# RWKV projections of keys, receptance, gate and values in products of Strassen's kind on one Trainium2 core

## The chip, the core and the metric

The kernel runs on one core of one Trainium2 chip. The metric is device time in microseconds, the median of three runs. Beside the runs there is one profiled execution, from which every trace row comes.

## The reference, cut to what matters

One step of a two-layer decoder. Layer 0 is an RWKV-7 layer; its input projection is what the change touches:

```python
proj = concat([prev_xn, xn]) @ w_in               # 1024 -> r, k, v (768 each), w/a LoRA, memory query, gate
mixed = cur + (proj[:, :-1, :n_sh] - cur) * mu     # token shift, for r, k, v
kk = k * k_k;  kk = kk / max(|kk|, 1e-12)          # per head of 64
k = k * (1 + (a - 1) * k_a)
S_t = S_{t-1} (diag(decay) - kk^T (kk a)) + v^T k;  o_t = S_t r_t
y = concat([norm(o) + bonus * v, memory]) * silu(gate);  h = h + y @ w_out
```

There are 1024 prompt tokens, 8 samples of 8 tokens and 8 carried rows, so the turned input `xT` is 128 partitions x 8 blocks of the 1024 inputs x 1096 columns (1024 + 64 + 8). All data are float32. After layer 0 come shared keys and values, a second layer of attention and the sample attention; the change does not touch them.

## The kernel before

`rwkv_pairs` handles the 12 heads as 6 pairs (`PAIRS`), each pair on the 128 partitions. A pair p has two phases on TensorE (PE), written out by hand:

- `middle(p)`: turn the values (`turn_tokens(0, vT)`), wait for `prep_ready`, then the decay products (line 833), which VectorE (DVE) masks, then five levels of small products that invert the chunks' triangular matrices.
- `recurrence(p)`: 16 steps n, one for each chunk of 64 tokens, a loop of dependences. In a step PE multiplies the state (line 1003), ScalarE (ACT) copies the result out as `r_sb` (line 1156), PE multiplies it (line 1020), DVE copies that out as `sa_sb` (line 1362), PE makes the next state (lines 1032 and 1033), and DVE writes it as `xs` (line 1368).

Between these dependent products PE fills in the projections of the next pair. The projections are a list of `PIECES`, each cut into `PARTS` (one matrix product of 128 inputs), dealt evenly over 48 slots, three to a step: slots 3n and 3n+1 follow line 1020's product, slot 3n+2 follows the new state's.

```python
PIECES = "W0 A0 K0 W1 A1 K1 W2 A2 K2 R0 R1 H0 R2 H1 V0 H2 V1 V2 G0 G1 G2".split()
                    fill(p + 1, 3 * n)
                    fill(p + 1, 3 * n + 1)
```

K, R, V, G are keys, receptance, values and gate, 8 parts each for the columns 0 to 384, 384 to 768 and 768 to 1096 (`COL3`); W and A are the two LoRA products; H sums squares for the norm of the keys. Each piece has one of four PSUM banks (piece i bank 4 + i % 4), and `wait_read` makes PE wait until the piece four before it has been read. ACT and DVE read the pieces in `feed(q, n)`, which each engine calls once at the end of step n: on ACT behind the copy of `r_sb` of step n, on DVE behind `xs` of step n (and at n == 7 behind the work of line 1380). In it ACT scales a piece by `mu` into `prev` (lines 1066 to 1070), and DVE adds the shifted columns (`mixed`, lines 1205 and 1207). Further work of `feed` stands at fixed n: the scan (line 1249) at 5, exponentials at 7, norms at 11 to 14, and at n == 15 the last two operations (lines 1275 and 1276), which raise `prep_ready`. SyncE (SP) loads the weights, 512 KB for each of K, R, V, G, into two halves of `w`: K and V into half 0, R and G into half 1. The first pair's projections run alone, ahead of `middle(0)`; pairs and recurrences are counted from 0, so recurrence 1 (312.6 to 405 us) fills in pair 2's projections; the last pair's recurrence fills in a list `TAIL` of other projections.

Of the kernel before, what the change touches and what calls it, by code (L numbers as in the profile page):

```python
# [14 lines left out]
F32 = mybir.dt.float32  # L15
# [5 lines left out]
P = 128  # L21
# [30 lines left out]
def make_constants():  # L52
# [27 lines left out]
    keep = np.ones(TT)  # L80
    keep[0:SEQ:HS] = 0
    keep[SEQ::TS] = 0
    put("keep", np.broadcast_to(keep, (P, TT)))
# [463 lines left out]
PIECES = "W0 A0 K0 W1 A1 K1 W2 A2 K2 R0 R1 H0 R2 H1 V0 H2 V1 V2 G0 G1 G2".split()  # L547
PARTS = [(i, k) for i, name in enumerate(PIECES) for k in range(KC if name[0] in "KRVG" else 1)]
# [20 lines left out]
def ended(step):  # L569

    return ended_in(step, FILL, PARTS, lambda i: KC - 1 if PIECES[i][0] in "KRVG" else 0)

# [6 lines left out]
def rwkv_pairs(nc, w_in, state_d, new_state_p, new_state_s, const, vecs, rows, omu, xT, wide, bank, lora, up, w, mq, y_m, y_last, y_d):  # L579
# [8 lines left out]
    with Stage(nc, "rwkv") as st:  # L588
# [9 lines left out]
        arT = st.sb("arT", [P, 2, NCHUNK, 2, CH])  # L598
# [28 lines left out]
        w_loaded = [st.sem(f"w_loaded{i}") for i in range(2)]  # L627
        (s0_loaded, hv_ready, piece_done, prev_ready, mix_read, th_read, h_read, g_tanh, gate_read, sq_ready, sig_ready,
# [61 lines left out]
        def _(sp):  # L690
            for q in range(PAIRS):
                for i, job in enumerate(JOBS):
                    if 4 * q + i < 2:
                        continue
                    qq, j = divmod(4 * q + i - 2, 4)
                    sp.wait_ge(piece_done, NPIECE * qq + PIECES.index(JOBS[j] + "2") + 1)
# [50 lines left out]
        def _(pe):  # L747
# [3 lines left out]
            def wait_read(q, i):  # L751
                kind, j = PIECES[i][0], int(PIECES[i][1])
                if kind in "KRV":
                    pe.wait_ge(mix_read, 9 * q + 3 * "KRV".index(kind) + j + 1)
# [4 lines left out]
                else:  # L759
                    pe.wait_ge(gate_read, 3 * q + j + 1)  # L760
# [2572 lines left out]
```

## Time and profile before

| | us |
|---|---|
| median of 3 runs | 2054.27 (2053.07 to 2056.26) |
| the profiled execution's own time | 2057.22 |
| its span, first to last instruction | 2055.3 |
| PE busy | 1912.8 (93%) |
| DVE busy | 963.2 (47%) |
| ACT busy | 635.1 (31%) |
| mean granted TensorE clock | 0.981 |

The RWKV stage lies between 77 us and about 937 us of the span: the first pair's projections from 77 to 142.5, then six times a middle of about 40 us and a recurrence of about 92 us. Busy shares are those of each engine; an engine's queue is served in its own order, so what counts is what is queued ahead of an instruction that PE needs.

### The profile page before, as it was taken

To read this page: it belongs to the slowest core of one execution; us is meant where nothing else is said; L and a number is where in the kernel's file an instruction comes from. 1 tells how busy PE (TensorE), PEld (TensorE's weight loads), DVE (VectorE), ACT (ScalarE), POOL (GpSimd) and SP (SyncE) were. 2 spreads that over 40 slices of the span, in tenths; PEclk is the share of its full clock that TensorE was granted. 3 is DMA by queue.
4 is the path that set the end of the run, shared out by engine and by line. 5 is a ranking of instruction groups with operands and counts; after the bars stand their busy time and mean duration, and the time that the engine had idled before them with its cause. 6 is when DMAs were issued, how large, how long until landed. Compare 5 with 4: busy or idle time off the path is not lost. (4 is left out here: it accounts for less than half of the span.)

```text
span 2055.3 us, 44993 instructions
## 1 busy us (share of the span) xinstructions
PE 1912.8 (93%) x19534; PEld 1314.8 (64%) x19534; DVE 963.2 (47%) x2083; ACT 635.1 (31%) x1499; POOL 305.1 (15%) x286
## 2 busy tenths in 40 slices
PE   6999989999999899897998999999999899799997
PEld 3577575675765757654443699995556566566664
DVE  4354373553734636332323476585233788633332
ACT  6322322222222223121224323232323566511111
POOL 0100030020300302111001010100010566201010
PEclk9999999999999999999999999999999999799998
DMA  8010010010100101007102130210200100667662
GB/s 290 18 37 3 22 34 23 18 39 22 34 23 12 45 22 34 24 17 263 57 1 107 53 116 32 96 52 11 92 22 11 62 1 1 236 201 231 214 223 77
DMA packets 53943, 147.70 MB, mean 72 GB/s; under 512 B 11587, under 2 KB 21123, under 8 KB 52468
## 3 DMA queue, kind: packets, MB, share of 16 engines
q1 hardware_dynamic: 43764, 103.97, 14.9%
q0 software_dynamic: 9984, 40.87, 5.7%
q8 instruction: 154, 2.52, 0.5%
q14 instruction: 41, 0.34, 0.1%
HBM read 123.58 MB, written 21.24 MB: 70 GB/s over the span
## 5 line engine op out<-in xcount | busy, mean ns | idle before, releaser
L772 PE MATMUL psum<-xT,rw_w 128*128 128x384 f32 (+1 forms) x1152 | 401.2, 487 | 0.0
L772 PEld LDWEIGHTS psum<-xT,rw_w 128*128 128x128 f32 x1152 | 205.7, 190 | 115.7 <-issue 10.7
L1368 DVE SCALAR_TENSOR_TENSOR rwkv_xs<-psum,rwkv_pc,rwkv_xsc 128x64 f32<-128x64 f32 x90 | 25.6, 284 | 225.2 <-PE psum L1033 225.2
L740 POOL DMA_DIRECT2D out<-rwkv_s x6 | 5.8, 960 | 638.5 <-ACT rwkv_out_p L1178 638.5
L1156 ACT COPY rwkv_r_sb<-psum 128x64 f32<-128x64 f32 x96 | 20.3, 212 | 258.4 <-PE psum L1003 256.0
L1625 PE MATMUL psum<-xT,gate_w 128*128 128x384 f32 (+1 forms) x288 | 97.3, 488 | 1.9 <-PEq L169 1.9
L1549 PE MATMUL psum<-xT,y_r 128*128 128x512 f32 (+1 forms) x180 | 87.2, 617 | 8.4 <-DMA y_r<-gated 8.4
L2904 PE MATMUL psum<-V,yT 128*128 128x512 f32 x192 | 92.7, 604 | 0.0
L3106 ACT COPY xT<-psum 128x384 f32<-128x384 f32 x64 | 30.5, 476 | 169.1 <-PE psum L3015 169.1
L3140 DVE COPY xT<-psum 128x384 f32<-128x384 f32 x64 | 35.6, 556 | 95.1 <-PE psum L3015 95.0
L919 PE MATMUL psum<-rwkv_dd,rwkv_am 64*64 64x64 f32 x1968 | 67.7, 219 | 9.8 <-issue 9.7
L1625 PEld LDWEIGHTS psum<-xT,gate_w 128*128 128x128 f32 x288 | 54.0, 195 | 35.0 <-issue 9.2
L2604 PE MATMUL psum<-KT,QT 64*128 64x512 f32 (+3 forms) x336 | 61.4, 479 | 14.1 <-ACT xT L2655 12.7
L919 PEld LDWEIGHTS psum<-rwkv_dd,rwkv_am 64*64 64x64 f32 x1968 | 62.8, 135 | 10.8 <-issue 10.8
L3015 PEld LDWEIGHTS psum<-base,kp 128*128 128x128 f32 x384 | 47.6, 148 | 34.1 <-issue 26.4
L1362 DVE COPY rwkv_sa_sb<-psum 128x64 f32<-128x64 f32 x96 | 21.6, 225 | 98.8 <-PE psum L1020 97.9
L801 PE MATMUL psum<-xT,rw_w 128*128 128x384 f32 (+1 forms) x192 | 66.7, 484 | 0.0
L1337 DVE TENSOR_TENSOR rwkv_mm<-psum,masks 128x256 f32<-128x256 f32 (+1 forms) x132 | 49.1, 396 | 33.1 <-PE psum L919 31.2
L1147 ACT COPY rwkv_dd<-psum 128x256 f32<-128x256 f32 (+1 forms) x108 | 37.1, 355 | 87.7 <-PE psum L934 69.2
L3015 PE MATMUL psum<-base,kp 128*128 128x128 f32 x384 | 57.4, 289 | 6.8 <-ACT xT L3106 3.9
L2615 PE MATMUL psum<-V,xT 128*128 128x128 f32 x432 | 62.5, 289 | 1.3 <-ACT xT L2677 1.3
L2615 PEld LDWEIGHTS psum<-V,xT 128*128 128x128 f32 x432 | 53.9, 193 | 12.7 <-issue 8.5
(514 smaller groups left out, 4136.3 us busy)
## 6 DMA issues: line engine op xcount, KB each, us to landing
kp<-in_cache_k SPq DMA_DIRECT2D x64, 384.0 KB, 4.0
xT<-in_cache_v POOLq DMA_DIRECT2D x48, 384.0 KB, 4.3
rw_w<-in_w_in SPq DMA_DIRECT2D x28, 512.0 KB, 3.6
gate_w<-in_cache_v POOLq DMA_DIRECT2D x16, 384.0 KB, 5.7
front_w<-in_mem_w_kv SPq DMA_DIRECT2D x2, 2048.0 KB, 14.5
x_rows<-in_x_p SPq DMA_DIRECT2D x8, 512.0 KB, 13.9
h<-in_x_p SPq DMA_DIRECT2D x8, 512.0 KB, 12.8
residual<-h POOLq DMA_DIRECT2D x8, 512.0 KB, 2.9
```

Of the source, the lines that this page charges most:

```text
L772: mm = pe.matmul(out, w[:, load % 2, k, :], xT[:, k, a:b], start=(k == 0), stop=(k == KC - 1))
L801: mm = pe.matmul(out, w[:, load % 2, k, :], xT[:, k, a:b], start=(k == 0), stop=(k == KC - 1))
L919: mm = pe.matmul(level_bank(g)[d, u, :], am[d, n, 0, :], dd[d, n, :], start=True, stop=True)
L1147: nc.scalar.copy(dd[:, group(g), :], level_bank(g)).then_inc(d_ready, 1)
L1337: nc.vector.tensor_tensor(mm_[:, group(g), :], level_bank(g), bcast(const_view(const, f"pair{b}").unsqueeze(1), [P, n, CH]), ALU.mult).the ...
L1549: mm = pe.matmul(self.bank[0:r, 5 + 2 * (u % 2), :], self.ys[k][:, n * P:n * P + r], self.w[:, k, half * 512:(half + 1) * 512], start=(k = ...
L1625: mm = pe.matmul(out, self.w[:, c % 2, k, :], self.xT[:, k, a:b], start=(k == 0), stop=(k == KC - 1))
L2604: mm = pe.matmul(both(m, is_big)[:, c, a:b], QT[d, h, i * P:(i + 1) * P], KT[d, h, a:b], start=True, stop=True)
L2615: mm = pe.matmul(bank[:, 7, 0:P], wT[:, j * P:(j + 1) * P], V[:, j, h * P:(h + 1) * P], start=(j == 0), stop=(j == i))
L2904: mm = pe.matmul(self.out(u), self.ys[k][:, n * P:(n + 1) * P], self.w[k][:, half * 512:(half + 1) * 512], start=(k == 0), stop=(k == KC - 1))
L3015: mm = pe.transpose(bank[:, 4 + half, i * P:(i + 1) * P], kp[:, g % KR, (H3 * half + i) * P:(H3 * half + i + 1) * P], ident[:, :])
L3140: nc.vector.tensor_copy(kT[:, g % TR, 1, :], bank[:, 5, 0:H3 * P]).then_inc(dve_out, 1)
```

## The change

For the first 768 tokens the pair (K, R), and then the pair (G, V), is computed as one 2 x 2 block product. The blocks are the two matrices on one side, by halves of the 1024 inputs, and on the other side the halves of the inputs by the two column ranges 0 to 384 and 384 to 768. Seven products of four parts each (X0 to X6, then Y0 to Y6) take the place of four plain pieces of eight parts each: 28 parts for 32. The columns from 768 on stay plain pieces (K2, R2, V2, G2). Sums of input blocks (`token_sums`) are made once; sums of weight blocks (`weight_sums`, `first_sum`) once for each product set and pair. Seven additions a set (`joins`) put the PSUM results together in SBUF.

The token shift of K, R and V for the 768 columns then runs from SBUF, after X6 or Y6, 768 columns at a time (`scaled_sums` on ACT, `mixed_sums` on DVE), and so do the gate's tanh and product. To make room, `arT` has one copy in place of two (its last chunks are written at n == 15), `masked` one half in place of two, the scan's mask is written anew for each pair, the keys and values of the memory (`mkT`, `mv`) are stored to DRAM at the start and loaded back at the end, and the block X12 of `xT`, which is overwritten by a difference, too.

```diff
-PIECES = "W0 A0 K0 W1 A1 K1 W2 A2 K2 R0 R1 H0 R2 H1 V0 H2 V1 V2 G0 G1 G2".split()
-PARTS = [(i, k) for i, name in enumerate(PIECES) for k in range(KC if name[0] in "KRVG" else 1)]
+PIECES = ("K2 R2 " + " ".join(f"X{j}" for j in range(7)) + " W0 A0 W1 A1 W2 A2 V2 H0 H1 H2 " + " ".join(f"Y{j}" for j in range(7)) + " G2").split()
+DEPTH_OF = {**{c: KC for c in "KRVG"}, **{c: KC // 2 for c in "XY"}}
+PARTS = [(i, k) for i, name in enumerate(PIECES) for k in range(DEPTH_OF.get(name[0], 1))]
...
         @block.sync
+            for d, t in zip(lent_d, lent):
+                sp.dma_start(d, t).then_inc(lent_out, 16)
+            sp.dma_start(lent_d[2].rearrange("p (k c) -> p k c", k=KH), X12).then_inc(lent_out, 16)
...
-                    qq, j = divmod(4 * q + i - 2, 4)
-                    sp.wait_ge(piece_done, NPIECE * qq + PIECES.index(JOBS[j] + "2") + 1)
+                    sp.wait_ge(piece_done, piece(q, "X6") if i >= 2 else piece(q - 1, ("Y6", "G2")[i]))
...
+                if i == 1:
+                    sp.wait_ge(lent_out, 48)
+                    sp.dma_start(X12, lent_d[2].rearrange("p (k c) -> p k c", k=KH)).then_inc(lent_back, 16)
+                    for d, t in zip(lent_d, lent):
+                        sp.dma_start(t, d).then_inc(lent_back, 16)
...
         @block.tensor
+                elif kind in "XY" and j == 0:
+                    pe.wait_ge(copied, 2 * q + 1 + "XY".index(kind))
+                elif kind in "XY":
+                    pe.wait_ge(joined, 14 * q + 7 * "XY".index(kind) + READ_BY[j])
...
+                    if k == 0 and j == 1:
+                        pe.wait_ge(sums_ready, 1)
+                        pe.wait_ge(factors_ready, n + 1)
+                    if k == 0 and j == 5:
+                        pe.wait_ge(first_ready, n + 1)
+                    left, right = product(kind, j, k)
+                    mm = pe.matmul(out, left, right, start=(k == 0), stop=(k == KH - 1))
...
         @block.scalar
+            def scaled_sums(q, kind, src, n):
+                act.wait_ge(joined, 14 * q + 7 * ("KRV".index(kind) // 2 + 1))
+                act.wait_ge(mix_read, 6 * q + n - 1)
+                nc.scalar.activation(prev[:, 1:1 + 2 * CW], src[:, 0:2 * CW], ACT.Copy, scale=vec(vecs, "mu", W_CHUNK[kind] + q)).then_inc(prev_ready, 1)
...
+                    elif PIECES[i] in ("X0", "Y0"):
+                        first_copy(q, i)
+                    elif PIECES[i] == "X6":
+                        scaled_sums(q, "K", kT, 3)
+                        scaled_sums(q, "R", rT, 4)
+                        act.wait_ge(mix_read, 6 * q + 3)
+                        nc.scalar.activation(kkT, kT[:, :], ACT.Square, scale=vec(vecs, "k_k", q)).then_inc(sq_ready, 1)
+                    elif PIECES[i] == "Y6":
+                        scaled_sums(q, "V", vT, 6)
+                        act.wait_ge(mix_read, 6 * q + 6)
+                        nc.scalar.activation(prev[:, 0:2 * CW], gT[q % 2][:, 0:2 * CW], ACT.Tanh, scale=0.5).then_inc(g_tanh, 1)
+                    if PIECES[i] == "A2":
+                        act.wait_ge(th_read, 6 * q + 5)
+                        nc.scalar.activation(sig[:, :], sig[:, :], ACT.Copy, scale=0.5, bias=0.5).then_inc(sig_ready, 1)
...
         @block.vector
+            def mixed_sums(q, kind, out, n):
+                s = omu[:, W_CHUNK[kind] + q:W_CHUNK[kind] + q + 1]
+                if kind == "K":
+                    dve.wait_ge(gate_read, 2 * q)
+                    link(nc.vector.memset(prev[:, 0:1], 0.0))
+                dve.wait_ge(prev_ready, 6 * q + n)
+                dve.wait_ge(mix_read, 6 * q + n - 1)
+                nc.vector.scalar_tensor_tensor(out=out[:, 0:2 * CW + 1], in0=out[:, 0:2 * CW + 1], scalar=s, in1=prev[:, 0:2 * CW + 1],
+                                               op0=ALU.mult, op1=ALU.add).then_inc(mix_read, 1)
...
+            def weight_sums(q, kind):
+                link(nc.vector.tensor_tensor(F3, one[:, 0:KH, :], two[:, 0:KH, :], ALU.subtract))
+                link(nc.vector.tensor_tensor(F2, two[:, KH:KC, :], F3, ALU.subtract))
+                for part in range(2):
+                    k = slice(2 * part, 2 * part + 2)
+                    ins = nc.vector.tensor_tensor(F4[part], one[:, KH + 2 * part:KH + 2 * part + 2, :], F2[:, k, :], ALU.subtract)
+                ins.then_inc(factors_ready, 1)
...
+                    if PIECES[i] == "A2":
+                        dve.wait_ge(sig_ready, q + 1)
+                        keep = const_view(const, "keep")
+                        nc.vector.tensor_copy(chunks(dinv), bcast(keep.unsqueeze(1), [P, NPC, CH]))
+                        link(nc.vector.tensor_copy(samples(dinv), bcast(keep[:, 0:TS].unsqueeze(1), [P, B, TS])))
+                        nc.vector.tensor_tensor_scan(cum[:, :], dinv[:, :], sig[:, :], 0.0, ALU.mult, ALU.add).then_inc(cum_ready, 1)
...
                 if n == 15:
+                    nc.vector.tensor_tensor(ar[:, 11:NPC, 1, :], chunks(rT)[:, 11:NPC, :], dec[:, 11:NPC, 1:CH + 1], ALU.mult)
+                    nc.vector.scalar_tensor_tensor(out=ar[:, NPC - 2:NPC, 0, :], in0=kkc[:, NPC - 2:NPC, :], scalar=-1.0,
+                                                   in1=dec[:, NPC - 2:NPC, 0:CH], op0=ALU.mult, op1=ALU.mult)
                     nc.vector.tensor_tensor(kaT[:, :], kaT[:, :], dinv[:, :], ALU.mult)
```

The other additions are one line each in kind: `token_sums` is three subtractions or additions of 1536 columns and two of 768, `first_sum` one addition of 512 (it needs R2 or V2 to be done), `first_copy` an ACT copy of 384, `joins` seven additions of 384 columns from PSUM for each set (X1, X2, X3, X4, X6 one, X5 two), and `tail_part` gains a wait for `lent_back`.

## Rows read from the trace of the kernel before

**Rows 1.** Windows: stretch; busy us (instructions) of PE, PEld, DVE, ACT, POOL; clock; DMA.
```profile
77.00:142.50 65.50, 65.50 (x212) 39.01 (x214) 25.76 (x39) 19.01 (x32) 6.06 (x4) 0.97 0.10 29
...
312.60:405.00 92.40, 90.97 (x869) 52.99 (x866) 34.75 (x88) 24.50 (x55) 0.64 (x1) 1.00 0.06 19
```

**Rows 2.** Waits of PE from 180 to 960 us: total, times, longest.
```profile
PE psum L1020 <- ACT rwkv_r_sb L1156: 9.4, 30, 1.1
```

**Rows 3.** Timeline of PE, fills of recurrence 1: start, duration, operation, count.
```profile
318.63 2.85 PE L772 MATMUL psum<-xT,rw_w 128*128 128x384 f32 x8
...
335.69 2.47 PE L772 MATMUL psum<-xT,rw_w 128*128 128x328 f32 x8
...
340.93 3.49 PE L772 MATMUL psum<-xT,rw_w 128*128 128x384 f32 x10
```

**Rows 4.** Timeline of PE, step 7 of recurrence 1.
```profile
352.47 0.33 PE L1020 MATMUL psum<-rwkv_r_sb,rwkv_ee 64*64 64x64 f32 x4
...
355.88 0.27 PE L1032 MATMUL psum<-rwkv_sa_sb,rwkv_am 64*64 64x64 f32 x1
...
356.15 1.37 PE L772 MATMUL psum<-xT,rw_w 128*128 128x328 f32 x4
...
358.21 0.33 PE L1020 MATMUL psum<-rwkv_r_sb,rwkv_ee 64*64 64x64 f32 x4 [0.20 <-ACT rwkv_r_sb L1156]
```

**Rows 5.** Timeline of DVE, step 7 of recurrence 1.
```profile
356.31 0.28 DVE L1368 SCALAR_TENSOR_TENSOR rwkv_xs<-psum,rwkv_pc,rwkv_xsc 128x64 f32<-128x64 f32 x1 [3.17 <-PE psum L1033]
...
357.38 0.68 DVE L1380 TENSOR_TENSOR rwkv_expd<-masks,rwkv_v_tok 128x512 f32<-128x512 f32 x1
357.98 0.61 DVE L1205 SCALAR_TENSOR_TENSOR spare<-psum,omu,rwkv_mm 128x384 f32<-128x384 f32 x1
```

**Rows 6.** Timeline of ACT, step 6 of recurrence 1.
```profile
346.63 0.21 ACT L1156 COPY rwkv_r_sb<-psum 128x64 f32<-128x64 f32 x1 [6.05 <-PE psum L1003]
...
346.84 0.60 ACT L1066 ACTIVATE rwkv_mm<-psum,vecs 128x384 f32<-128x384 f32 x1
347.31 1.21 ACT L1114 ACTIVATE rwkv_dd<-spare,vecs 128x1088 f32<-128x1088 f32 x1
```

**Rows 7.** Timeline of PE, first pair of W and A in recurrence 1.
```profile
321.69 0.92 PE L780 MATMUL psum<-lora,up 64*128 64x384 f32 x4
322.53 0.91 PE L772 MATMUL psum<-xT,rw_w 128*128 128x384 f32 x2
```

**Rows 8.** Timeline of DVE and PE, end of recurrence 1 and start of middle 2.
```profile
402.98 0.28 DVE L1368 SCALAR_TENSOR_TENSOR rwkv_xs<-psum,rwkv_pc,rwkv_xsc 128x64 f32<-128x64 f32 x1 [1.87 <-PE psum L1033]
...
404.85 1.29 DVE L1276 SCALAR_TENSOR_TENSOR rwkv_beT<-rwkv_beT,rwkv_dinv 128x1088 f32<-128x1088 f32 x1
...
406.70 0.39 PE L833 MATMUL psum<-rwkv_arT,rwkv_beT 64*64 64x128 f32 x4
```

**Rows 9.** Timeline of DVE and PE, steps 13 and 14 of recurrence 1.
```profile
396.59 0.23 DVE L1362 COPY rwkv_sa_sb<-psum 128x64 f32<-128x64 f32 x1
...
397.39 0.27 PE L1032 MATMUL psum<-rwkv_sa_sb,rwkv_am 64*64 64x64 f32 x1
```

**Rows 10.** Timeline of PE, end of the first pair's projections.
```profile
142.41 2.08 PE L749 MATMUL psum<-base,y_m 64*64 64x64 f32 x64
144.32 0.39 PE L833 MATMUL psum<-rwkv_arT,rwkv_beT 64*64 64x128 f32 x4
```

**Rows 11.** Timeline of PE from 76.98 us, with the idle time before.
```profile
76.98 1.21 PE L780 MATMUL psum<-lora,up 64*128 64x384 f32 x4 [2.76 <-PEq L169]
78.12 6.78 PE L772 MATMUL psum<-xT,rw_w 128*128 128x384 f32 x16
...
85.67 5.43 PE L772 MATMUL psum<-xT,rw_w 128*128 128x384 f32 x16
```

**Rows 12.** Windows of the same stretch; PEclk stands before DMA share and GB/s.
```profile
79.00:80.00 1.00, 1.00 (x3) 0.59 (x2) 1.00 (x4) 0.00 (x0) 1.00 (x1) 0.50 0.00 0
...
81.00:82.00 1.00, 1.00 (x5) 0.60 (x4) 0.11 (x5) 0.91 (x2) 0.93 (x1) 1.00 0.00 0
```

More of the change, by code:

```diff
@@ L1196, in mixed @@
             def mixed(q, i):
[L1197 removed]
+                kind = PIECES[i][0]
                 m = "KRV".index(kind)
@@ new lines, in weight_sums @@
+            def weight_sums(q, kind):
+                one, two = sides_of(kind)
+                n = 2 * q + "XY".index(kind)
+                if n >= 1:
+                    for side in range(2):
+                        dve.wait_ge(w_loaded[side], 16 * n)
+                    dve.wait_ge(piece_done, piece(q, "X6") if kind == "Y" else piece(q - 1, "Y6"))
+                else:
+                    dve.wait_ge(lent_out, 48)
+                link(nc.vector.tensor_tensor(F3, one[:, 0:KH, :], two[:, 0:KH, :], ALU.subtract))
[4 more added lines that the diff above has]
+                ins.then_inc(factors_ready, 1)
@@ new lines, in first_sum, with token_sums @@
+            def first_sum(q, kind):
+                one, two = sides_of(kind)
+                dve.wait_ge(piece_done, piece(q, "R2" if kind == "X" else "V2"))
+                dve.wait_ge(factors_ready, 2 * q + 1 + "XY".index(kind))
+                nc.vector.tensor_tensor(two[:, 0:KH, :], two[:, 0:KH, :], two[:, KH:KC, :], ALU.add).then_inc(first_ready, 1)
+            def token_sums():
+                x11, x21, x22 = xT[:, 0:KH, 0:CW], xT[:, KH:KC, 0:CW], xT[:, KH:KC, CW:2 * CW]
+                link(nc.vector.tensor_tensor(U3, x22, X12, ALU.subtract))
+                link(nc.vector.tensor_tensor(U2, U3, x11, ALU.add))
+                dve.wait_ge(lent_out, 48)
+                nc.vector.tensor_tensor(X12, X12, x11, ALU.subtract)
+                for part in range(2):
+                    k = slice(2 * part, 2 * part + 2)
+                    ins = nc.vector.tensor_tensor(U4[part], x21[:, k, :], U2[:, k, :], ALU.subtract)
+                link(ins)
+                dve.sem_inc(sums_ready, 1)
@@ L3226, in build @@
                       (sh_p, sh_s))
-            rwkv_pairs(nc, i["w_in"], i["state"], st_p, st_s, const, vecs, rows, omu, xT, wide, bank, lora, up, rw_w, mq, y_m, y_last, y_d)
+            rwkv_pairs(nc, i["w_in"], i["state"], st_p, st_s, const, vecs, rows, omu, xT, wide, bank, lora, up, rw_w, mq, y_m, y_last, y_d,
+                       [t[:, :, :, :].rearrange("p a b m -> p (a b m)") for t in (mkT, mv)], lent_d)
         late = sb("late", [P, _CONST[2].shape[1]])
```

185 lines of the change are left out of this document (119 added, 66 removed).

## The prediction

> **What bounds the kernel now.** I read the busy shares by stage first. Both in the first pair's projections and in a recurrence PE is busy without a break (65.5 of 65.5 us, 91.0 of 92.4 us) and DVE and ACT are at 40% or less [rows 1]. Then the waits: through the whole RWKV stage PE waits only 9.4 us for `r_sb`, 1.1 us at most at a time [rows 2]. So PE's own work sets the time, and a part taken from the fills is worth its full time, as long as the two short answers that a step needs, `r_sb` from ACT and `sa_sb` from DVE, come before PE has used up its fills. Third, the timelines of single steps: they show how much room those answers have, and what each engine does before it gives them. That is where this change must be read, for it moves the readers of the pieces into chains that go from ACT to DVE and back.
>
> **What it removes.** Two more instructions make a fill of 384 columns 0.64 us longer (3.49 against 2.85 us), and four parts of 328 take 0.38 us less than four of 384, so a part costs 0.64 or 0.545 us, and a change of work about 0.2 us [rows 3]. A pair has 32 parts of 384 less 28, in each of two sets: 8 x 0.64 = 5.1 us less on PE. Over six pairs that is 31 us, if nothing new is waited for.
>
> **The slots.** 97 parts in 48 slots put X6's last part into slot 21, the first fill of step 7; W0 and A0 into slot 22, W1 and A1 into 23, W2 and A2 into 24; V2 into 25 to 28; Y0 begins in 30, Y6 ends in 44 (read at step 15), G2 in 47.
>
> **Step 7, the X chain.** I take recurrence 1's step 7 and count in its own times. PE's product at 352.47, then fills, new state at 355.88 [rows 4]. Now the fills are two X parts (1.28) and the pair W0, A0 (0.84 from start to start, [rows 7]) instead of two of 384 and three of 328 (2.92), so the new state comes at 355.1, and DVE's `xs` at 355.5, with the same 0.43 behind it as before. DVE then does line 1380's work, 1.67 us from `xs` to the next item [rows 5]: free at 357.2. What follows is serial, each waiting for the one before: X6's addition of 384 from PSUM (between 0.51, three quarters of the 0.68 of 512 columns, and the 0.61 of line 1205, both [rows 5]; I take 0.55); ACT scales 768 of K; DVE mixes 769 of K; ACT scales R only then, since both use `prev`; then the square of 1088; then the tanh of W0 and A0; and only then, in ACT's order, `r_sb` of step 8. ACT's 768 lie between 0.60 for 384 and 1.21 for 1088 [rows 6]: 0.92. DVE's 769 lie between 0.61 for 384 [rows 5] and 1.29 for 1088 [rows 8]: 1.0. So 357.2 + 0.55 + 0.95 + 1.03 + 0.95 + 1.1 + 2 x 0.5 + 0.2 = 363.0. Left alone, step 8's product would start at 355.1 + (358.21 - 355.88) - 1.09 + 0.84 = 357.2, two parts of 328 in slot 23 being replaced by W1 and A1 [rows 4, 7]. PE waits 5.8 us for `r_sb`, with nothing else it may do; A1's wait for X6's bank (X6 must be added first, 357.8) falls inside it. Bounds: 4.5 us if every 768 goes at the low end, 6.5 at the high. Before, nothing of ACT's work in a step waited for DVE's work in the same step, so this wait is new.
>
> **Steps 15 and 16, the Y chain.** At the end of a recurrence nothing fills. With T for `xs` of step 15 (402.98), PE starts the decay products at 406.70, T + 3.7 [rows 8]. Now DVE adds Y6 (to T + 0.75), ACT scales V (1.7), DVE mixes V (2.75), ACT takes the tanh of 768 (3.6), DVE forms the gate (4.6), writes the last chunks of `arT` (320 and 128 columns; from 0.4 to 0.8 us, I take 0.6: 5.2), and then the two 1088-column operations, 1.2 apart, the second ending at T + 7.6, where `prep_ready` lets PE go. So 3.9 us later than before. PE's turning of the values, which waits for V, and ACT's copies lie inside this (T + 2.75 to about 5.2). The masking behind it shifts as a whole. Bounds: 3.0 and 4.6.
>
> **The rest of DVE's new work** lies under PE's fills. At step 14 `sa_sb` was ready 0.6 us before PE used it [rows 9]; Y3 and Y4 at step 13 are two additions of 0.55 where one gate operation of that length stood: 0 to 0.8 us, 0.4 taken. At step 8 DVE writes the mask (a 1024 copy, from 0.7 to 1.3 us by the widths above) ahead of the scan; at step 9 it mixes V2, makes the weight sums (2.2 us at 0.68 per 512, [rows 5]) and `first_sum` (0.65), 3.9 us with V2's mixing. DVE has from `xs` of a step to the use of `sa_sb` in the next: PE's own products, 1.7 us (5.74 from product to product less 4.0 us of parts, [rows 4]), and six parts, so 5.0 us with parts of 328 and 5.6 with parts of 384. Both steps' work just fits under that. If it does not, it costs up to 1.5 us a pair, which I keep for the range. The V and G loads start at X6, and V2 comes four slots later, behind the wait above: hidden. Copies of X0 and Y0 on ACT (0.5) fall in quiet steps. `masked` in halves is the same work. The last recurrence has no X or Y; the reload of `mkT`, `mv` and X12 on SP has a whole middle of some 40 us before tail part two needs it.
>
> One steady pair: - 5.1 + 5.8 + 3.9 + 0.4 = + 5.0 us; five of them, + 25 us.
>
> **The first pair** runs with no recurrence. It saves 5.1, and pays in three places. Before X1, DVE makes the token sums, free from 81 [rows 12]: three of 1536 and two of 768 (about 1.8 and 0.95 each, scaled from the 1.29 of 1088, [rows 8]) and the X weight sums, so X1 starts at 90.6, where PE with K2, R2, X0 arrives at 90.2. The three stores of 1.8 MB must land within 7 us for that; DMA is otherwise nearly idle there [rows 1]; no row shows them, 0 to 4 us, I take 0. Then W2 waits for W0's tanh, behind the same X chain on ACT: about 4 us. Y0 and Y1 wait for V2's mixing, behind the mask and the scan, about 1 us. PE ends G2 about where it did, 142.4 [rows 10], but the Y chain and the `arT` remainder put `prep_ready` at about 146.3 against the decays' 144.32 [rows 10]. Sum + 2 us, range - 1 to + 6.
>
> **The clock.** After 2.76 us without work at 74 us, the granted clock is 0.50 (1.2 GHz) around 79 to 80 and 1.00 (2.4 GHz) again from 81, and the first K piece took 6.78 us, the second 5.43 [rows 11, 12]: a drop costs about 1.35 us there, 1.7 with the W and A before it. The new wait leaves PE without work for about 3.7 us in one piece before step 8, after a sparse second; the one at the recurrence's end comes in pieces of 2 us or so. I take 1 us a pair for five pairs, + 5; ends 0 and 3.4 a pair. *TensorE: Matmul & The Clock Gate* of the Trainium skill, "HAM oscillation — how this bites in real kernels", says that a wait which is repeated in each pass lets the clock fall to half each time, and that each pass then starts cold; by it every one of the ten waits would pay. For one wait the trace agrees, with its clock of 0.50 [rows 12].
>
> **Sum.** 25 + 2 + 5 = + 32 us on the profiled execution's 2057.2 us (span 2055.3), which lies 2.9 us above the median of the runs, 2054.3. Against the median: 2086 us. A measurement of this kernel can tell about 0.2%, 4 us, from no change.
>
> **Rivals.** (1) *The clock falls at both waits of every pair.* For it: the one drop that the trace shows came after 2.76 us [rows 11, 12], and both waits are longer. Against: short products lie in the second. 10 x 1.7 = 17 us in place of 5: 2098 us. Chance 0.15. The Trainium skill's *TensorE: Matmul & The Clock Gate* would have it this way, by the section named above. (2) *Only the X chain shows.* If the gate and V in the last steps finish under G2's seven parts (3.9 us in slots 44 to 47), `prep_ready` comes little later. For it: Y6 itself is done on PE before step 15's product. Against: DVE takes it up only behind `xs` of step 15. 5 x (- 5.1 + 5.8 + 0.4) + 2 + 5 = + 12.5: 2067 us. Chance 0.1. (3) *The parts saved show in full*, the other side: one mechanism, that ACT's `r_sb` of step 8 is not held up, because X6 is added and scaled while PE still has fills. The point where it decides is 357.2 in step 8: the chain would have to end 5.8 us earlier than I count. For it: PE waits hardly at all today [rows 2], ACT and DVE are at 40% or less. Against: the order on ACT, with DVE's 1.67 us ahead of it in that very step. If it holds and the Y chain costs its 3.9: 5 x (- 5.1 + 3.9 + 0.4) + 2 = - 2: 2052; if neither shows, 5 x - 5.1 + 2 = - 23.5: 2031. Chance 0.1 for the two.
>
> My forecast has 0.65: its own range 2074 to 2097. Low end of the whole: rival 2 with the low waits, 2062; high end: rival 1 and the uncovered work of steps 8 and 9, 2102. What is left outside is about 0.2. Faster by over 0.2% has 0.07, within 0.2% 0.05, slower 0.88.
>
> **What the profile after would show.** PE's group of projection products falls by 96 instructions (two for each of 48 parts), some 31 us of work; the wait of line 1020's product for `r_sb` grows from 9.4 to some 38 us, in five waits of 5 to 6; `prep_ready` in each of five middles about 3.9 us later behind the last `xs`, seen as PE idle before line 833's products; DVE busy some 80 us more. A recurrence grows from 92.4 to about 94.5 us. I would be wrong if the waits for `r_sb` stay short, if V's chain is done at an earlier step than 15, or if the granted clock lies well under 1.00 across the stage.

## The result, and the profile after

The changed kernel takes 2106.05 us (median of 4 runs, 2104.68 to 2110.72), the kernel before 2054.98 in the same session: a ratio of 1.0253, 95% interval 1.0235 to 1.0272, so 51 us slower. The forecast was 2086 us with a range up to 2102: right in direction and in the two delays that it worked out, too small by 20 us in all, 4 us outside the range. On the profiled executions it is 49.9 us of span (2105.2 against 2055.3); the forecast has 32.

The page of the changed kernel, span and busy time:

```profile
span 2105.2 us, 45135 instructions
...
PE 1914.0 (91%) x19438; PEld 1316.1 (63%) x19438; DVE 1052.1 (50%) x2250; ACT 633.2 (30%) x1487; POOL 306.6 (15%) x286
```

PE has its 96 instructions fewer, as forecast, and yet it is busy 1.2 us longer than before (1912.8): a part that runs at half clock takes longer (A1's below: 1.64 us for 0.91). The mean granted clock is 0.966, before 0.981. DVE has 89 us more. The waits of PE from 193 to 893 us, the five steady pairs (total, times, longest):

```profile
PE psum L1074 <- ACT rwkv_r_sb L1223: 20.4, 25, 3.8
PE psum L886 <- DVE rwkv_beT L1424: 11.9, 5, 2.4
...
PE psum L831 <- DVE spare L1299: 7.6, 5, 1.5
...
PE psum L783 <- DVE y_m L1284: 5.3, 5, 1.1
...
PE psum L1086 <- DVE rwkv_sa_sb L1511: 2.6, 5, 0.5
```

Before, `r_sb` was the one answer of another engine that PE waited for here [rows 2]; now there are five such rows. Line 831 is the product of the W and A pieces, here A1's, which waits for X6's bank; L1074 is step 8's product; L783 the turning of the values in the middle, L886 the first decay product.

The X chain in the timelines of step 7 of recurrence 1, DVE, ACT and PE, beside [rows 4, 5]:

```profile
371.26 0.28 DVE L1517 SCALAR_TENSOR_TENSOR rwkv_xs<-psum,rwkv_pc,rwkv_xsc 128x64 f32<-128x64 f32 x1 [2.24 <-PE psum L1087]
...
372.92 0.55 DVE L1299 TENSOR_TENSOR spare<-spare,psum 128x384 f32<-128x384 f32 x1
...
374.52 1.02 DVE L1284 SCALAR_TENSOR_TENSOR spare<-spare,omu,rwkv_mm 128x769 f32<-128x769 f32 x1 [1.05 <-issue]
376.61 1.02 DVE L1284 SCALAR_TENSOR_TENSOR spare<-spare,omu,rwkv_mm 128x769 f32<-128x769 f32 x1 [1.06 <-ACT rwkv_mm L1132]
...
373.50 0.94 ACT L1132 ACTIVATE rwkv_mm<-spare,vecs 128x768 f32<-128x768 f32 x1 [5.33 <-DVE spare L1299]
375.64 0.94 ACT L1132 ACTIVATE rwkv_mm<-spare,vecs 128x768 f32<-128x768 f32 x1 [1.20 <-DVE spare L1284]
376.48 1.19 ACT L1177 ACTIVATE rwkv_dd<-spare,vecs 128x1088 f32<-128x1088 f32 x1
...
378.50 0.21 ACT L1223 COPY rwkv_r_sb<-psum 128x64 f32<-128x64 f32 x1
...
373.52 1.64 PE L831 MATMUL psum<-lora,up 64*128 64x384 f32 x2 [1.52 <-DVE spare L1299]
...
378.75 0.48 PE L1074 MATMUL psum<-rwkv_r_sb,rwkv_ee 64*64 64x64 f32 x4 [2.76 <-ACT rwkv_r_sb L1223]
```

From `xs` to PE's product it is 7.5 us, as the forecast has it (355.5 to 363.0), and the links have about the lengths taken there. In the same stretch the granted clock (the column behind POOL busy; then DMA share and GB/s):

```profile
372.00:374.00 2.00, 0.48 (x2) 0.48 (x2) 1.47 (x4) 0.50 (x1) 0.00 (x0) 0.79 0.98 377
374.00:380.00 6.00, 3.24 (x22) 1.52 (x21) 2.43 (x4) 4.80 (x9) 0.00 (x0) 0.50 0.05 19
380.00:382.00 2.00, 2.00 (x7) 1.05 (x4) 0.00 (x0) 1.51 (x4) 0.00 (x0) 0.50 0.00 0
382.00:384.00 2.00, 2.00 (x19) 1.01 (x19) 0.17 (x1) 0.57 (x1) 0.00 (x0) 0.65 0.00 0
384.00:386.00 2.00, 2.00 (x52) 1.41 (x50) 1.97 (x4) 0.21 (x1) 0.00 (x0) 1.00 0.00 0
```

TensorE falls from 2.4 to 1.2 GHz while it waits and stays there until 383.3, 4.6 us after `r_sb` has come: A1, W2, A2 and the first parts of V2 run at half speed. In steps of half a microsecond the fall lies in 373.0 to 373.5, so already inside A1's wait of 1.5 us, ahead of the longer one. It is so in four of the five pairs (A1 then takes 1.64 us, and the wait for `r_sb` is 2.8); in recurrence 0 A1 still runs at full clock (0.91), the wait is 3.8, and the fall comes inside it.

The new work of step 13 shows once a pair, in step 14 (before: no such wait):

```profile
418.09 0.27 PE L1086 MATMUL psum<-rwkv_sa_sb,rwkv_am 64*64 64x64 f32 x1 [0.52 <-DVE rwkv_sa_sb L1511]
```

The Y chain at the end of the same recurrence, DVE and PE, beside [rows 8]:

```profile
423.68 0.28 DVE L1517 SCALAR_TENSOR_TENSOR rwkv_xs<-psum,rwkv_pc,rwkv_xsc 128x64 f32<-128x64 f32 x1 [1.08 <-PE psum L1087]
...
427.36 0.96 DVE L1378 SCALAR_TENSOR_TENSOR rwkv_gT<-rwkv_mm,rwkv_gT 128x768 f32<-128x768 f32 x1 [0.91 <-ACT rwkv_mm L1181]
...
430.04 1.28 DVE L1424 SCALAR_TENSOR_TENSOR rwkv_beT<-rwkv_beT,rwkv_dinv 128x1088 f32<-128x1088 f32 x1
...
431.38 0.69 PE L886 MATMUL psum<-rwkv_arT,rwkv_beT 64*64 64x128 f32 x4 [2.38 <-DVE rwkv_beT L1424]
```

The decay products start at T + 7.7 (forecast 7.6, before 3.7). With them the clock is at 0.50 again:

```profile
432.00:434.00 2.00, 2.00 (x23) 2.00 (x21) 1.70 (x4) 0.00 (x0) 0.78 (x1) 0.50 0.38 85
```

All five middles show this, and all five recurrences the drop of step 7 (before: one drop of the clock in the five pairs). The first pair, DVE, GpSimd and PE, beside [rows 11]:

```profile
78.42 3.73 DVE L1259 TENSOR_SCALAR rwkv_hv<-vecs 128x6 f32<-128x6 f32 x1
...
82.21 2.68 DVE L1325 TENSOR_TENSOR rwkv_u_own<-xT 128x1536 f32<-128x1536 f32 x1
84.92 2.53 DVE L1326 TENSOR_TENSOR rwkv_u_own<-rwkv_u_own,xT 128x1536 f32<-128x1536 f32 x1
87.49 1.76 DVE L1328 TENSOR_TENSOR xT<-xT 128x1536 f32<-128x1536 f32 x1
...
78.23 3.90 POOL L766 MEMSET rwkv_am<- 128x4352 f32 x1
82.19 1.09 POOL L767 COPY rwkv_am<-masks 128x1088 f32<-128x1088 f32 x1
83.23 2.61 POOL L768 COPY rwkv_first<-masks 128x1088 f32<-128x1088 f32 x1
...
93.49 5.70 PE L823 MATMUL psum<-rwkv_u_own,rwkv_f_own 128*128 128x384 f32 x12 [3.74 <-DVE mv L1314]
```

Equal operations of 1536 columns take 2.68, 2.53 and 1.76 us: the first two run beside GpSimd's copies. The waits of PE there (L823 is X1, L831 W2, L886 the first decay product), and its start:

```profile
PE psum L831 <- ACT rwkv_sig L1137: 3.8, 1, 3.8
PE psum L823 <- DVE mv L1314: 3.7, 1, 3.7
PE psum L810 <- PEq L166: 2.8, 1, 2.8
PE psum L886 <- DVE rwkv_beT L1424: 2.6, 1, 2.6
...
78.10 9.07 PE L810 MATMUL psum<-xT,rw_w 128*128 128x328 f32 x32 [2.76 <-PEq L166]
```

The forecast had 0.4 at X1.

**Where the 51 us are.** The start of DVE's state updates (`xs`) marks each step in every trace. The table gives the start of the stage on PE (the instruction behind the wait of 2.76 us) and the first `xs` of recurrence 0, both from the span's start; the means over recurrences 0 to 4 of first to last update, of the step from 7 to 8, and of the middle behind it (last update to the next recurrence's first); a whole pair; and the time of the kernel. All in us.

| kernel | stage starts | first `xs` | recurrence | step 7 to 8 | middle | pair | kernel |
|---|---|---|---|---|---|---|---|
| before | 77.0 | 183.1 | 86.8 | 5.3 | 45.1 | 131.9 | 2054.98 |
| after | 78.1 | 194.0 | 90.2 | 12.6 | 49.6 | 139.8 | 2106.05 |
| e1 clock kept | 76.9 | 189.2 | 88.1 | 10.4 | 48.4 | 136.5 | 2084.19 |
| e2 Y chain off | 76.6 | 186.0 | 90.4 | 12.6 | 46.5 | 136.9 | 2083.69 |
| e3 X chain off | 78.4 | 188.0 | 84.2 | 5.3 | 49.4 | 133.6 | 2070.73 |
| e4 both off | 77.0 | 182.0 | 84.2 | 5.3 | 45.9 | 130.0 | 2047.44 |
| e5 GpSimd later | 77.3 | 188.9 | 90.2 | 12.5 | 49.6 | 139.8 | 2100.62 (one run) |
| e6 before, eight parts less | 78.2 | 178.8 | 82.4 | 5.3 | 44.8 | 127.2 | 2026.94 |
| e7 e4 with three moves | 78.1 | 184.2 | 83.9 | 5.3 | 45.2 | 129.1 | 2040.37 |
| e8 square later | 78.4 | 191.3 | 89.4 | 11.5 | 50.5 | 139.9 | 2102.42 (one run) |

After less before: 11.0 up to the first `xs`, of which 1.1 are only the later start of the stage, 7.9 in each of five steady pairs (39.5), and nothing in the last recurrence (70.95 against 70.96 us). The stage's start moves by up to 1.8 us between traces, in no order that an edit explains, so first pairs are compared from there.

### The profile page after: what moved, and what is told of

Its sections match the earlier page's. It is cut to its first block and busy times, and to the rows that moved or that the text cites. A ratio compares the mean times of both kernels' runs of the same rounds, so it can differ in the third digit from the quotient of the medians.

```text
span 2105.2 us, 45135 instructions
## 1 busy us (share of the span) xinstructions
PE 1914.0 (91%) x19438; PEld 1316.1 (63%) x19438; DVE 1052.1 (50%) x2250; ACT 633.2 (30%) x1487; POOL 306.6 (15%) x286
## 5 line engine op out<-in xcount | busy, mean ns | idle before, releaser
L810 PE MATMUL psum<-xT,rw_w 128*128 128x328 f32 x384 | 128.3, 475 | 2.8 <-PEq L166 2.8
L823 PE MATMUL psum<-xT,rw_w 128*128 128x384 f32 x288 | 108.5, 503 | 0.0
L810 PEld LDWEIGHTS psum<-xT,rw_w 128*128 128x128 f32 x384 | 72.2, 199 | 37.2 <-issue 6.1
L823 PE MATMUL psum<-rwkv_u_own,rwkv_f_own 128*128 128x384 f32 x192 | 72.9, 513 | 4.4 <-DVE mv L1314 3.7
L2753 PE MATMUL psum<-KT,QT 64*128 64x512 f32 (+3 forms) x336 | 61.3, 480 | 14.0 <-ACT xT L2804 12.6
L823 PEld LDWEIGHTS psum<-xT,rw_w 128*128 128x128 f32 x288 | 51.0, 190 | 28.7 <-DVE y_m L1274 0.4
L854 PE MATMUL psum<-xT,rw_w 128*128 128x384 f32 (+1 forms) x192 | 66.7, 485 | 0.0
```

What stands on the lines that cost most here:

```text
L810: mm = pe.matmul(out, w[:, load % 2, k, :], xT[:, k, a:b], start=(k == 0), stop=(k == KC - 1))
L823: mm = pe.matmul(out, left, right, start=(k == 0), stop=(k == KH - 1))
L854: mm = pe.matmul(out, w[:, load % 2, k, :], xT[:, k, a:b], start=(k == 0), stop=(k == KC - 1))
L2753: mm = pe.matmul(both(m, is_big)[:, c, a:b], QT[d, h, i * P:(i + 1) * P], KT[d, h, a:b], start=True, stop=True)
```

## The experiments

The kernel before took 2052.72 us (13 runs) beside e1 to e4 and 2056.43 (9 runs) beside e5 to e8, and 2054.98 beside the changed kernel. So a difference to the changed kernel's 2106 us holds to some 2 us only; taken against the kernel before of its own session, e1 gains 20 us, e2 20, e3 33, e4 56 and e7 67.

**e1, the clock kept.** No wait is taken away; PE gets idle work in the waits.

```diff
+            def keep_busy(b, count):
+                for _ in range(count):
+                    pe.matmul(bank[:, b, 256:384], ident, xT[:, 7, 0:P], start=True, stop=True)
...
+                if PIECES[i] == "A1" and q >= 1:
+                    keep_busy(0, 6)
+                if q == 0 and k == 0:
+                    keep_busy(3, {"X1": 16, "W2": 14, "Y1": 2}.get(PIECES[i], 0))
...
+                if p >= 1:
+                    keep_busy(0, 4)
                 pe.wait_ge(mix_read, 6 * (p + 1))
...
+                keep_busy(7, 10)
                 pe.wait_ge(prep_ready, p + 1)
...
                     mm.then_inc(r_mm, 1)
+                    if n == 8 and p < PAIRS - 1:
+                        keep_busy(3, 12)
```

> Changed kernel with TensorE kept busy in the waits: 12 matmuls of 128 columns into unused columns before the new-state work of step 8, 6 ahead of the A1 part, 4 and 10 in the middle ahead of the two waits there, and 16, 14, 2 and 10 at four waits of the first pair; no wait is taken away. Theory (waits cost 5.8 and 3.9 us a pair, and the clock that falls behind them another 2 and 1.3): the clock stays at 1.0 behind the waits, the step from 7 to 8 falls from 12.5 to about 10.5 us, a pair from 139.8 to about 136.5, and the kernel from 2106 to about 2088 with some 3 us of the first pair. Rival 1 (the clock is a mere sign and costs nothing of its own, the waits are longer than worked out): the granted clock is higher but the time stays at 2106 or rises by up to 3 us by the added matmuls. Rival 2 (a clock that fell for another reason than the wait): the clock falls all the same and the time stays.

2084.19 us (2079.44 to 2088.21), 1.0161 of before (1.0139 to 1.0183), so about 20 us less than the changed kernel, where 18 were expected. The windows of e1 over the same step of recurrence 1:

```profile
364.50:366.50 2.00, 2.00 (x14) 1.63 (x14) 1.46 (x4) 0.52 (x1) 0.00 (x0) 1.00 1.01 414
366.50:372.50 6.00, 5.19 (x47) 4.02 (x46) 2.43 (x4) 4.80 (x10) 0.00 (x0) 1.00 0.04 18
372.50:374.50 2.00, 2.00 (x22) 1.22 (x22) 0.29 (x2) 1.96 (x4) 0.00 (x0) 1.00 0.00 0
```

The clock stays at 1.00 through all the recurrences and middles; DVE and ACT do the same work in the same time (2.43 and 4.80 us in the six-microsecond window, to the digit). The step falls by 2.1 us, the middle by 1.2, and the first pair by 3.6 from the stage's start (112.3 for 115.9 us): 5 x 3.3 + 3.6 = 20. The lower clock is a cost of its own, not a sign of the waits. In the first pair it is more than 3.6, for the 16 idle matmuls there last beyond the wait: X1 starts 16.7 us behind the stage's start, 15.4 without them. And what is left in a steady pair is the price of the waits alone: a pair is 4.6 us longer than before, where the forecast's sum without the clock says 5.0.

**e2, the Y chain off.** The values' blocks are complete after Y5, so they need not wait for Y6; the gate need not come ahead of `prep_ready`.

```diff
-                    elif PIECES[i] == "Y6":
+                    elif PIECES[i] == "Y5":
                         scaled_sums(q, "V", vT, 6)
+                    elif PIECES[i] == "Y6":
+                        act.wait_ge(joined, 14 * (q + 1))
                         act.wait_ge(mix_read, 6 * q + 6)
...
+                if n == 15:
+                    mixed_sums(q, "V", vT, 6)
                 for i in ended(n):
...
-                        if PIECES[i] == "Y6":
-                            mixed_sums(q, "V", vT, 6)
-                            dve.wait_ge(g_tanh, 2 * q + 1)
-                            nc.vector.scalar_tensor_tensor(out=gT[q % 2][:, 0:2 * CW], in0=prev[:, 0:2 * CW], scalar=1.0, in1=gT[q % 2][:, 0:2 * CW],
-                                                           op0=ALU.add, op1=ALU.mult).then_inc(gate_read, 1)
...
                                                    op1=ALU.mult).then_inc(prep_ready, 1)
+                    dve.wait_ge(g_tanh, 2 * q + 1)
+                    nc.vector.scalar_tensor_tensor(out=gT[q % 2][:, 0:2 * CW], in0=prev[:, 0:2 * CW], scalar=1.0, in1=gT[q % 2][:, 0:2 * CW],
+                                                   op0=ALU.add, op1=ALU.mult).then_inc(gate_read, 1)
```

> Changed kernel with the chain behind Y6 taken off: the values, complete after Y5, are scaled in step 14 and mixed at the head of step 15, and the gate's product over the first 768 tokens is put behind the four preparing operations. Theory (this chain delays the decay products by 3.9 us a pair and costs 1.3 of clock): the wait of the decay product on beT goes, the middle falls from 49.5 to about 44.3 us, the kernel from 2106 to about 2077 (5.2 x 5, and 3 in the first pair). Rival (VectorE is simply full in steps 14 to 16; the same work in another order only moves the wait to the third decay product, which needs the gate, or to the end of step 14): the middle stays above 48 us and the kernel above 2098.

2083.69 us (2082.88 to 2086.23), 1.0160 of before (1.0143 to 1.0177), about 20 us less than the changed kernel where 29 were expected. The scaling of the values then waits for two joins fewer. The wait on `beT`, 2.4 us before each middle, falls to 0.5, and no middle shows a lower clock any more:

```profile
PE psum L886 <- DVE rwkv_beT L1423: 2.5, 5, 0.5
```

The middle falls by 3.0 us, not by 5.2. The mix of the values at the head of step 15 still stands ahead of `prep_ready`; in e7, where it is moved, the wait on `beT` is gone. The recurrence stays as it was, so the two chains are separate. The first `xs` comes 8 us sooner, of which 1.5 are the start of the whole stage.

**e3, the X chain off.**

```diff
-                    elif PIECES[i] == "X6":
-                        scaled_sums(q, "K", kT, 3)
-                        scaled_sums(q, "R", rT, 4)
-                        act.wait_ge(mix_read, 6 * q + 3)
-                        nc.scalar.activation(kkT, kT[:, :], ACT.Square, scale=vec(vecs, "k_k", q)).then_inc(sq_ready, 1)
+                    elif PIECES[i] == "X5":
+                        scaled_sums(q, "R", rT, 3)
+                    if PIECES[i] == "A0":
+                        scaled_sums(q, "K", kT, 4)
...
+                if n == 9 and q < PAIRS:
+                    act.wait_ge(mix_read, 6 * q + 4)
+                    nc.scalar.activation(kkT, kT[:, :], ACT.Square, scale=vec(vecs, "k_k", q)).then_inc(sq_ready, 1)
...
-                        if PIECES[i] == "X6":
-                            mixed_sums(q, "K", kT, 3)
-                            mixed_sums(q, "R", rT, 4)
+                        if PIECES[i] == "X5":
+                            mixed_sums(q, "R", rT, 3)
...
+                if n == 8:
+                    mixed_sums(q, "K", kT, 4)
...
                     if n == SP_SA:
+                        feed(p + 1, n)
                         dve.wait_ge(sas_mm, p + 1)
```

> Changed kernel with the chain behind X6 taken off: receptance, complete after X5, is scaled and mixed in step 6; the keys are scaled behind W0 and A0 in step 7, mixed at the head of step 8, and squared in step 9; the sample state's work of step 7 goes behind the join. Theory (the chain holds up r_sb of step 8 by 5.8 us and costs 2 of clock): the step from 7 to 8 falls from 12.5 to about 5, a pair by 7.7, the kernel from 2106 to about 2067; the wait for r_sb falls from 20 us to about 9. Rival (ScalarE and VectorE are full in steps 6 to 9 and the delay only spreads): the steps 6, 8 and 9 grow by what step 7 gives back, and the kernel stays above 2090.

2070.73 us (2066.14 to 2071.98), 1.0087 of before (1.0071 to 1.0104), some 33 us less than the changed kernel, where 39 were expected. The step from 7 to 8 is back at 5.3 us and the clock stays at 1.00 in every recurrence; the A1 wait is gone, and the wait for `r_sb` is 12.8 us in all in the stretch where it was 20.4 (about 9 were expected):

```profile
PE psum L1074 <- ACT rwkv_r_sb L1225: 12.8, 33, 1.1
```

Steps 8 and 9 hardly grow (5.25 and 5.47 us against 5.10 and 5.47). Only step 6 to 7 does, by 1.0 us, since ACT now scales receptance just ahead of `r_sb`. The rival, that the delay only spreads, falls. e3 moves four pieces of work at once; e8 takes one of them alone.

**e4, both off.** The edits of e2 and e3 together.

> Both of the other two edits together. Theory: the gains add, 7.7 + 5.2 a pair and 3 in the first pair: 2106 - 67 = 2039, faster than the kernel before by 15 us: the eight saved parts (5.1 us a pair) show where the two chains are off, less the 11 us of the first pair. Rival (the saved parts are worth less than 0.64 us each, or some of the work only moves): no faster than the kernel before, 2055 or above.

2047.44 us (2042.64 to 2054.67), 0.9976 of before (0.9961 to 0.9992). The waits of PE from 193 to 893 us:

```profile
PE psum L1074 <- ACT rwkv_r_sb L1227: 14.2, 35, 1.1
PE psum L972 <- issue: 9.6, 10, 1.3
PE psum L987 <- issue: 7.8, 7, 1.5
PE psum L783 <- issue: 4.5, 5, 1.4
PE psum L1086 <- DVE rwkv_sa_sb L1516: 2.6, 5, 0.5
PE psum L886 <- DVE rwkv_beT L1426: 2.5, 5, 0.5
```

Faster than the kernel before, by 5 us where 15 were expected (1.6 to 8 by the interval). The ten runs spread over 12 us, and the trace is of one near their low end (2043.1), 14 us under the traced execution of the kernel before; so what follows from the rows says where the time is, and the medians how much it is in all. Against the changed kernel some 56 us are gone (67 expected). From the stage's start the first pair takes 105.1 us, 1 less than before and 10.9 less than changed; X1 starts as late in it as in the changed kernel (15.4 us), so these 10.9 are the two chains and the clock. A steady pair has 1.8 us less than before, not 5.1. Against e6, with as many parts and no chains, it is 2.9 us longer: 1.8 in the recurrence, half of it in step 6 to 7, and 1.1 in the middle, of which 0.5 is what is left of the wait on `beT`.

**e5, GpSimd later.**

```diff
             link(nc.gpsimd.memset(stat[:, 2, :], -0.5))
+            pool.wait_ge(sums_ready, 1)
             link(nc.gpsimd.memset(am[:, :, :, :], 0.0))
```

> Changed kernel in which GpSimd's clearing of the masks and its two copies begin only when the sums over the tokens are done. Theory (the two token sums that took 2.68 and 2.53 us beside GpSimd's work, where the third took 1.76 alone, are slowed by it): all three take about 1.76, TensorE's wait ahead of X1 falls from 3.7 to about 2 us, and the first state update of the first recurrence comes 2 us sooner than 194.0. Rival (they are slow for another reason, such as the three stores that run at the same time): they stay at 2.5 and more, and the wait stays at 3.7.

One execution, 2100.62 us. DVE, PE and PE's start in e5:

```profile
77.63 0.16 DVE L1260 TENSOR_SCALAR rwkv_hv<-vecs 128x6 f32<-128x6 f32 x1
...
78.03 1.76 DVE L1326 TENSOR_TENSOR rwkv_u_own<-xT 128x1536 f32<-128x1536 f32 x1
79.83 1.76 DVE L1327 TENSOR_TENSOR rwkv_u_own<-rwkv_u_own,xT 128x1536 f32<-128x1536 f32 x1
85.59 1.76 DVE L1329 TENSOR_TENSOR xT<-xT 128x1536 f32<-128x1536 f32 x1 [4.00 <-DMA lent<-xT]
...
91.59 5.40 PE L824 MATMUL psum<-rwkv_u_own,rwkv_f_own 128*128 128x384 f32 x16 [0.94 <-DVE mv L1315]
...
77.31 10.76 PE L811 MATMUL psum<-xT,rw_w 128*128 128x328 f32 x32 [2.77 <-PEq L166]
```

All three sums take 1.76 us, the theory's number (the rival, that the stores slow them, falls), and the tiny operations ahead of them 0.16 us in place of 3.73. DVE gains 5.1 us by that, and then gives 4.0 of them back in a wait for the stores of the lent tiles, which nothing had shown before. So X1 starts 14.3 us behind the stage's start and no longer 15.4: 1.1 us are gained. X1's wait falls by more, from 3.7 to 0.9 us, because PE comes later: its first 32 instructions take 10.76 us here and 9.07 in the changed kernel, with a granted clock of 0.50 from 78 to 81 us. That drop follows the wait of 2.76 us ahead of the stage, which every trace has; it comes in before, e1, e2, e4, e5 and e6, and does not come in after, e3, e7 and e8. The first `xs` is 5.1 us sooner where 2 were expected: 0.8 are the stage's start, 1.1 X1, 1.7 the drop that lies under DVE's sums here and behind X1 in the changed kernel, and 1.5 are open.

**e6, the kernel before with eight parts less a pair.**

```diff
-PARTS = [(i, k) for i, name in enumerate(PIECES) for k in range(KC if name[0] in "KRVG" else 1)]
+DEPTH_OF = [(KC if name[1] == "2" else KC - 1) if name[0] in "KRVG" else 1 for name in PIECES]
+PARTS = [(i, k) for i in range(len(PIECES)) for k in range(DEPTH_OF[i])]
```

> Kernel before, with the last of the eight 384- column parts left out in the first two blocks of each of the four projections: eight parts fewer a pair, as many as the change saves, and nothing else changed; the projections lack an eighth of their depth for the first 768 tokens. Theory (each part is 0.64 us on the path that sets the end, and nothing hides it): 5.1 us for each of six pairs, 31 in all, so 2024 where the kernel before has 2054; the recurrences fall from 86.8 to about 82.3 us, and the rest shows in the middles and in the first pair. Rival (the waits for r_sb and xs in each step take up part of it, so that the saving was never to be had in full): 2035 or above.

2026.94 us (2021.28 to 2028.69), 0.9843 of before (0.9825 to 0.9861): 29.5 us for 48 parts, 0.61 us each against 0.64 taken. Recurrences of 82.4 us, as expected (82.3). The saving that the change was counted with is there to be had. (The kernel leaves out an eighth of the depth, so it measures time only.)

**e7, e4 with three moves.**

```diff
                     link(nc.vector.scalar_tensor_tensor(out=beT[:, :], in0=aT[:, :], scalar=1.0, in1=kkT, op0=ALU.add, op1=ALU.mult))
+                    mixed_sums(q, "V", vT, 6)
                 if n == 15:
...
                     if n in (0, 6):
                         if n == 6:
+                            feed(p + 1, n)
                             dve.wait_ge(rs_mm, p + 1)
```

(with e5's line, and the mix at the head of step 15 taken out)

> The version with both chains off, and three small moves: the join behind X5 ahead of the sample state's mask in step 6, the mix of the values at the end of step 14 and no longer at the head of 15, and GpSimd's clearing behind the token sums. Theory (what is left of the waits is the 1.1 us for r_sb in step 7, 0.5 ahead of the decay product and 0.3 ahead of it at the second half of the turns, and GpSimd's share of the wait at X1): another 1.7 us a pair and 1.7 in the first, so 2047 - 10 = 2037. Rival (these stand already beside other waits): 2047, no better than the version without them.

2040.37 us (2038.90 to 2043.32, 5 runs), 0.9917 of before (0.9903 to 0.9931), 16 us faster than the kernel before; the interval lies clear of e4's. A pair has another 0.9 us less, not 1.7: step 6 to 7 falls from 6.2 to 5.6, but the mix in step 14 makes PE wait for `sa_sb` (10 times 0.4 us in 193 to 893, in e4 5 times 0.5), and step 14 to 15 grows from 5.2 to 5.5. GpSimd's line lets X1 start 14.1 us behind the stage's start, 15.4 in e4, with DVE held 3.85 us for the stores, as in e5. The first pair is no shorter by it (106.1 us against 105.1): in e4 the clock drops once at the stage's start, under DVE's sums, in e7 once behind X1, where it shows.

**e8, one link moved.**

```diff
-                        act.wait_ge(mix_read, 6 * q + 3)
-                        nc.scalar.activation(kkT, kT[:, :], ACT.Square, scale=vec(vecs, "k_k", q)).then_inc(sq_ready, 1)
...
+                if n == 9 and q < PAIRS:
+                    act.wait_ge(mix_read, 6 * q + 3)
+                    nc.scalar.activation(kkT, kT[:, :], ACT.Square, scale=vec(vecs, "k_k", q)).then_inc(sq_ready, 1)
```

> Changed kernel with one link of the chain behind X6 moved: the square of the keys is made in step 9 and no longer between the two scalings and r_sb of step 8. Theory (r_sb of step 8 stands behind ScalarE's own queue, so each link of that queue shows with its duration): the square is the 1.19 us link, but the mix of receptance, tanh of W0 and A0 stand behind it too, so r_sb comes 1.2 us sooner, the step from 7 to 8 falls from 12.5 to 11.3 and the kernel by 5 to 8 us. Rival (r_sb of step 8 waits for its product, which stands behind VectorE's work, and not for ScalarE's queue): the step stays at 12.5.

One execution. The step falls from 12.6 to 11.5 us: a link on ACT shows with about its length (1.1 of 1.19), so it is ACT's order of work that holds up `r_sb`, not PE's own product. The kernel's 2102.42 us lie 4 under the changed kernel's (5 against the kernel before of each session), the low end of what was expected, and the pairs are no shorter, as the middles were 0.9 us longer here. That is within what middles do without any edit: those of the kernel before range from 43.9 to 46.4 us, by PE's waits that no engine ends (listed as issue).

## Why the forecast was too low

- **The parts saved, - 5.1 a pair.** Right: 4.9 a pair by e6 (29.5 over six).
- **The X chain, + 5.8.** Right as a delay. The product comes 7.5 us behind `xs`, as worked out. It does not all show as a wait for `r_sb`: 1.5 us of it is A1's wait for X6's bank, and part of the rest is PE's own work at half clock. So the claim of 38 us in waits of 5 to 6 was wrong as a mark to look for (20.4 us in the five pairs, 3.8 at most), though the delay was right. e3 takes away the chain and the recurrence falls by 6.0 us, with the 1.0 that it adds at step 6.
- **The Y chain, + 3.9.** Right at the place: T + 7.7 against 7.6. In the middle as a whole e1, with the clock kept, has 3.3 us more than before.
- **Steps 8, 9 and 13, + 0.4.** Right: PE waits 0.5 us for `sa_sb` once a pair, in step 14, and not at all in steps 8 and 9 (5.1 and 5.5 us against 6.3 and 6.1 before).
- **A steady pair without the clock: + 5.0 forecast, + 4.6 in e1.**
- **The clock, "I take 1 us a pair".** This is the first step that failed. e1 puts it at 3.3 us a pair (2.1 behind the X chain, 1.2 behind the Y chain) and at least 3.6 in the first pair, for which the clock term had nothing: some 20 us in all against 5. The forecast argued from the one drop of before, took the new waits for only partly able to cause one, and held the short products in the second wait for a help; they were none: the granted clock is 0.50 behind both waits in all five pairs. That is rival 1, which had 0.15, and its 17 us for ten waits are what e1 measured (16.4 for the five pairs), though not 1.7 at each wait but 2.1 and 1.2. Rival 1 alone gives 2098 us, so the first pair was needed too to leave the range. The Trainium skill, *TensorE: Matmul & The Clock Gate*, "HAM oscillation — how this bites in real kernels", says that a wait repeated in each pass makes each pass start cold; the trace agrees, with ten drops in five pairs.
- **The first pair, + 2.** The second step that failed: + 11.0. Of these 1.1 are the later start of the stage in that trace, no cost of the change. X1 was to start 13.6 us behind the stage's start and starts 15.4: 1.8 later, and 1.7 of it is the two token sums that took 2.68 and 2.53 us in place of 1.76 beside GpSimd's copies. (e5 gives back 1.1 only, since the stores, for which the forecast took 0, then hold DVE; they are second in line, and hidden by the first.) The wait at X1 is longer by more than that, 3.7 us for 0.4, since PE was ready after 11.7 us and not after 13.2: the drop of the clock that before has at the stage's start did not come in this trace. W2's wait was right (3.8, forecast about 4). The rest is the clock: windows of one microsecond show three drops behind X1's, W2's and the decay products' waits, 5.1 us of full speed lost, where the forecast had one, at the start. 2 + 1.1 + 1.8 + 5.1 = 10.0; the last 1.0 us is open.
- **Rival 2** (only the X chain shows) falls by the middles and by e2, **rival 3** (the saved parts in full) by the changed kernel's own rows, where `r_sb` comes only at 378.5. With the X chain off it had - 2 us and e3 has + 18; with both off it had - 23.5 and e4 has - 5, faster but not by the parts saved in full.
- **The chances.** The forecast's 0.65 and the rivals' 0.15, 0.1 and 0.1 add up to 1.00, which leaves none of the 0.2 that it says lie outside its range; the result fell there.

Sum on the profiled executions: 5 x 4.6 + 16.4 + 11.0 = + 50.4 up to the last recurrence's first `xs`, and 0.5 less behind it: + 49.9.

Not settled: why PE's waits without a releaser make the middles differ by up to 2.5 us from one to the next, and which 0.8 us of e4's middle belong to them.

## What to carry to other kernels

Fewer multiplications pay only if reading the partial results does not hold up the next short answer: here all of it was put behind the last piece, as one chain between ScalarE and VectorE ahead of what TensorE waits for, at some 13 us a pair, the clock with it, for 5 saved. Read a result when it is complete; receptance and the values were so one piece before the last. Sort the work behind the last piece by who is queued behind it, and put what nobody waits for, such as a square or a gate, behind the answers. Where a wait of several microseconds on TensorE returns in each pass, count the half clock behind it as a cost beside the wait, here a third as much again. And compare stages from their own start: a wait on TensorE can shrink because TensorE was slower before it.

## What the hardware showed that was not expected

- **VectorE and GpSimd hold each other up.** Four operations of 6 columns ended 3.7 us after the first began, with GpSimd's clearing of 4352 columns (3.90 us), and took 0.16 us each without it (e5). Two sums of 1536 columns with two inputs took 2.68 and 2.53 us between GpSimd's copies and 1.76 without them, while a copy of 1088 took GpSimd 2.61 us between them and 1.08 in the kernel before, which has no such sums. The Trainium skill, *SBUF — State Buffer*, "SBUF: two separate sides", says that the two engines share one pair of ports, and that, where a VectorE operation is in a two-port mode, or has two SBUF inputs beside a GpSimd operation that reads SBUF, the one that comes second is held for the whole of the other's instruction. The trace agrees: the second operation of each pair ends its own length, less some 0.15 us, after the end of the first. Both sums end 1.61 us after the copy ahead of them, and the copy 0.95 us after the sum ahead of it.
- **The same wait does not always lower the clock.** The 2.76 us without work ahead of the stage are followed by a granted clock of 0.50 in six of the ten traces and by 1.00 in four (after, e3, e7, e8); at A1 the clock fell within a wait of 1.5 us in four of five pairs.
- **Work with no use pays.** Up to 32 idle matmuls in a pair, in waits that stay as they are, give back 3.3 us a pair by the granted clock alone (e1).
